# Attention, recurrence and a mixture of experts in one program: column halves at the end of each expert layer, row blocks for the input weights, expert rounds inside the pipeline, and a recurrent output product that starts with the front rows

## What is computed

```
h = x
for layer in (0, 1):
    hn = rms_norm(h, norm_mix[layer])
    h += attention(hn) if layer == 0 else recurrence(hn)
    h += mixture_of_experts(rms_norm(h, norm_ffn[layer]))
return rms_norm(h, final_norm)
```

## Time and profile before

| | us |
|---|---|
| median of 3 runs (lowest to highest) | 772.02 (771.46 to 773.8) |
| the profiled execution's own time | 769.73 |
| its span | 768.0 |
| PE busy | 641.2 (83%) |
| DVE busy | 315.9 (41%) |
| ACT busy | 224.2 (29%) |
| DMA, mean over the span | 321 GB/s, 246.15 MB |

### The profile page before, as it was taken

The page is one execution under the profiler, slowest core; times in us unless marked ns, Lnnn a source line. Parts: engine busy times, 40 slices in busy tenths (PEclk is TensorE's granted clock), DMA queues, the critical chain, the costliest instruction groups (busy, mean ns, idle before and its releaser), DMA issues.

```text
span 768.0 us, 11907 instructions
## 1 busy us (share of the span) xinstructions
PE 641.2 (83%) x4946; PEld 448.4 (58%) x4946; DVE 315.9 (41%) x533; ACT 224.2 (29%) x483; POOL 36.9 (5%) x62
## 2 busy tenths in 40 slices
PE   7999897999997595685879999989999985685775
PEld 6987786797453341331269999979965441332312
DVE  5555777545132211201375787742443311201204
ACT  4424654521121010110146666551211110110102
POOL 5100000000000100000000000050000000000000
PEclk9999999999999888987979999998999997987979
DMA  9993336578999999999993655529789999999993
GB/s 304 248 381 130 110 111 236 215 265 332 419 420 404 411 420 421 423 422 421 401 386 134 219 159 199 186 88 417 291 328 423 419 421 421 422 421 422 422 416 134
DMA packets 62580, 246.15 MB, mean 321 GB/s; under 512 B 4496, under 2 KB 12928, under 8 KB 41280
## 3 DMA queue, kind: packets, MB, share of 16 engines
q1 hardware_dynamic: 60896, 242.33, 80.5%
q0 software_dynamic: 992, 2.40, 1.0%
q10 hardware_dynamic: 640, 0.67, 0.3%
HBM read 244.34 MB, written 1.05 MB: 320 GB/s over the span
## 4 chain that ended last, share of the span: by engine, by line
PE 52%; DMA 28%; SPq 8%; DVE 6%; ACT 3%; issue 2%; DVEq 0%; ACTq 0%
DMA ring<-in_moe_w_down 19%; PE psum L2016 8%; PE psum L1673 8%; DMA ring<-in_moe_w_up 7%; PE psum L2073 7%; PE psum L1675 5%; PE psum L1682 4%; SPq L388 4%; PE psum L1684 3%; PE psum L1677 3%; SPq L437 2%; PE psum L2009 2%; PE psum L2000 2%; DMA ring<-in_att_w_in 2%; SPq L445 1%
## 5 line engine op out<-in xcount | busy, mean ns | idle before, releaser
L1421 DVE TENSOR_TENSOR arena<-psum,arena 128x256 f32<-128x256 f32 x16 | 6.8, 425 | 219.6 <-ACT arena L927 219.6
L2016 PE MATMUL psum<-arena,xT 128*32 128x512 f32 x512 | 64.7, 663 | 38.1 <-DMA arena<-in_moe_w_up 38.1
L2016 PE MATMUL psum<-ring,xT 128*32 128x512 f32 x512 | 66.4, 678 | 34.0 <-DMA ring<-in_moe_w_up 34.0
L2073 PE MATMUL psum<-ring,arena 128*32 128x512 f32 x464 | 59.4, 607 | 12.0 <-DMA ring<-in_moe_w_down 11.0
L1673 PE MATMUL psum<-x_hi,w_hi 128*128 128x256 f32 x256 | 65.8, 294 | 1.3 <-DVE x_hi L1110 0.6
L349 DVE TENSOR_TENSOR w_lo<-ring,w_hi 128x1024 fp32r<-128x1024 f32 x48 | 57.1, 1221 | 23.3 <-ACT w_hi L724 23.3
L923 ACT ACTIVATE arena<-psum 128x256 f32<-128x256 f32 x16 | 6.1, 383 | 207.1 <-PE psum L2016 207.1
L2016 PEld LDWEIGHTS psum<-arena,xT 128*32 128x32 f32 x512 | 17.7, 120 | 80.5 <-issue 45.2
L724 ACT ACTIVATE w_hi<-ring 128x1024 fp32r<-128x1024 f32 x48 | 49.0, 1052 | 47.7 <-PE psum L1684 28.1
L2016 PEld LDWEIGHTS psum<-ring,xT 128*32 128x32 f32 x512 | 17.0, 122 | 77.4 <-issue 42.2
L2009 PE MATMUL psum<-arena,xg 128*128 128x128 f32 x512 | 60.3, 276 | 0.7 <-DVE arena L1408 0.7
(11 more groups left out here) (313 smaller groups left out, 1037.9 us busy)
## 6 DMA issues: line engine op xcount, KB each, us to landing
ring<-in_moe_w_down SPq DMA_DIRECT2D x58, 1024.0 KB, 20.5
ring<-in_moe_w_gate SPq DMA_DIRECT2D x32, 1024.0 KB, 17.5
ring<-in_moe_w_up SPq DMA_DIRECT2D x32, 1024.0 KB, 19.6
arena<-in_moe_w_gate SPq DMA_DIRECT2D x32, 1024.0 KB, 23.1
arena<-in_moe_w_up SPq DMA_DIRECT2D x32, 1024.0 KB, 24.7
ring<-in_rec_w_in SPq DMA_DIRECT2D x16, 1024.0 KB, 13.6
ring<-in_att_w_in SPq DMA_DIRECT2D x8, 1024.0 KB, 12.7
ring<-in_att_w_out SPq DMA_DIRECT2D x4, 1024.0 KB, 10.6
```

Of the source, the lines that this page charges most:

```text
L2016: return pe.matmul(bank(3)[e * CAP:(e + 1) * CAP, :].rearrange("p (w f) -> p w f", w=2), gatheredT[:, k, e * CAP:(e + 1) * CAP], w, start= ...
L2073: last = pe.matmul(bank(5 + c)[e * CAP:(e + 1) * CAP, :], hidT[:, j, e * CAP:(e + 1) * CAP], down_part(l, kind, e, j)[:, c * 512:(c + 1) * ...
```

## The change

1. **Row blocks.** `cols` and the new `keys_values` give partition p the rows p, p+128, ... of the weight. The norms of the layers' inputs (v = 0 and 2) and the final one write straight; only the experts' norms keep the stride.
2. **Keys, values and gates** arrive as one block of 792 adjacent columns over two ring slots, in four DMAs. Their split waits for both slots. The low part of the `WG` columns moves to `ahead`, its split is two pieces on ACT and DVE instead of one, and the load of `U_VB` waits for three used units instead of two.
3. **First product.** DVE makes both low parts of `x` before the first low part of the weights; `first_quarter` starts with high x high when the first high part is there.
4. **Rounds.** `more` is read before the pipeline's loop on PE and ACT, whose loops now run to the last quad of the last round; the `If` of PE and ACT is gone. DVE and SP keep one, ahead of the last two (DVE) or the last (SP) quad.
5. **End of an expert layer.** `turn_hidden` of the last quad stands before the combine of the one before it. `down` signals its front half of columns (`down_front`) apart; `combine` goes by column half, then by row block, and starts with `y_front`. ACT squares each half of each row block as its adds finish (`norm_by_halves`); the first half's mean goes in as the bias of the logarithm.
6. **Recurrent output product.** For row block 0 DVE makes the high part too; PE runs the tile (0, 0) between the transposes of row block 0 and of row block 1. The order is then (1, 0), (0, 1), (1, 1), and m = 2, 3 as before.

```diff
 def cols(w, c0, n):
-    v = w.rearrange("(p k) n -> p k n", k=KD)[:, :, c0:c0 + n]
+    v = w.rearrange("(k p) n -> p k n", p=P)[:, :, c0:c0 + n]
...
+def keys_values(k0):
+    v = att.rearrange("(k p) n -> p k n", p=P)[:, :, C_KC:C_KC + KVW]
+    return [(lambda r, i=i: kvw[:, i:i + 2, :], v[:, i:i + 2, :]) for i in (k0, k0 + 2)]
-plan = [cols(att, 0, 512), blocks(512, (C_KC, 3 * P), (C_KW, P)),
-        blocks(WG, (C_VS, P), (C_VW, WG - P)),
+plan = [cols(att, 0, 512), keys_values(0), keys_values(KD // 2),
+RING_NEEDED[U_VB] = RING_NEEDED[U_WO]
...
 # DVE, norm
-if v < 2 * NL:
+if v % 2:
     rows = rows.rearrange("p (j k) -> p j k", k=KD)
 # PE
+def first_quarter(dst):
+    pe.wait_ge(s["w_high"], 1)
+    for k in range(KD):
+        pe.matmul(dst, quarter_hi(0)[:, k, :], x_hi[:, k, :], start=(k == 0), stop=False)
+    pe.wait_ge(s["x_lo_done"], TT)
+    for k in range(KD):
+        pe.matmul(dst, quarter_hi(0)[:, k, :], x_lo[:, :, k, :], start=False, stop=False)
+    pe.wait_ge(s["w_low_dve"], 1)
+    for k in range(KD):
+        last = pe.matmul(dst, q_lo[:, 0, k, :], x_hi[:, k, :], start=False, stop=(k == KD - 1))
...
 # PE, experts
+pe.wait_ge(s["passes_ready"], l + 1)
+more = pe.value_load(passes[l][0:1, 0:1], min_val=0, max_val=PASS_MAX - 1)
-with pe.Fori(2, NQ // 2) as i:
+with pe.Fori(2, (more + 1) * (NQ // 2)) as i:
     body(l, 2 * i, 0)
     body(l, 2 * i + 1, 1)
-pe.wait_ge(s["passes_ready"], l + 1)
-more = pe.value_load(passes[l][0:1, 0:1], min_val=0, max_val=PASS_MAX - 1)
-pe.wait_ge(s[f"added{l}"], 4 * NQ - 4)
-combine(l, NQ - 2)
-turn_hidden(l, NQ - 1)
-down(l, NQ - 1, last_quad=True)
-combine(l, NQ - 1)
+end = NQ * more + NQ - 1
+turn_hidden(l, end)
+pe.wait_ge(s[f"added{l}"], 4 * end)
+combine(l, end - 1)
+down(l, end, last_quad=True)
+pe.wait_ge(s[f"added{l}"], 4 * end + 4)
+combine(l, end)
 if l == 0:
     keep_clock(NORM, 3)
-with pe.If(more > 0):
-    with pe.Fori(0, more) as r:
...
 # PE, combine
-pe.wait_ge(s[f"y_rows{l}"], 2 * m + 2)
 for i, b in enumerate(COMBINE_BANKS):
-    t, half = divmod(i, 2)
+    half, t = divmod(i, 2)
+    if t == 0:
+        pe.wait_ge(s[f"y_back{l}" if half else f"y_front{l}"], m + 1)
...
 # ACT
+def norm_by_halves(l):
+    v = 2 * l + 2
+    for half in range(2):
+        for t in range(TT):
+            act.wait_ge(s["h_done"], H_NEEDED[v] + 2 * half + t + 1)
+            link(act.activation(square_moe[:, 0:512], h[:, t, half * 512:(half + 1) * 512], ACT.Square,
+                                accum_out=norm_part[:, l, t, half:half + 1]))
+            if half:
+                rstd(v, t, norm_part[:, l, t, 1:2], norm_part[:, l, t, 2:3])
+            else:
+                link(act.activation(norm_part[:, l, t, 2:3], norm_part[:, l, t, 0:1], ACT.Identity,
+                                    bias=eps_col[:, 0:1], scale=1.0 / D))
...
 # DVE, recurrence, inside the loop over row blocks, after the scaling of block t
+if t == 0:
+    for b in (0, 1):
+        dve.wait_ge(s["recT_psum"], b + 1)
+        dve.tensor_copy(rec_turned(mix_hi, b), bank(b).rearrange("p (k t) -> p k t", k=4))\
+            .then_inc(s["recT_high"], 1)
+    for b in (0, 1):
+        turned_low(b)
...
 # PE, recurrence, after the two transposes of row block t
+if t == 0:
+    pe.wait_ge(s["recT_high"], 2)
+    mix_tile(1, BASE_REC + 8, REC_BANKS, 0, (s["recT_low"], 2))
```

More of the change, by code:

```diff
@@ L566, in _ @@
                     with sp.Fori(0, more) as r:
[L567 to L573 removed]
+                        later_quad(NQ * r + NQ - 1, NQ - 1, 1, NQ - 2)
+                        later_quad(NQ * r + NQ, 0, 0, NQ - 1)
+                        with sp.Fori(0, NQ // 2 - 1) as i:
+                            n = NQ * (r + 1) + 2 * i
+                            later_quad(n + 1, 2 * i + 1, 1, 2 * i)
+                            later_quad(n + 2, 2 * i + 2, 0, 2 * i + 1)
+                end = NQ * more + NQ - 1
+                later_quad(end, NQ - 1, 1, NQ - 2)
+                sp.wait_ge(s[f"gate_up{l}"], end)
+                load_last_down(sp, l)
             for t in range(TT):
@@ L697, in hybrid_trunk @@
         COMBINE_BANKS = (7, 2, 0, 1)
-        H_NEEDED = [None, (7, 8), (10, 12), (19, 20), (22, 24)]
+        MIX_ORDER = ([(m, t) for m in range(4) for t in range(TT)],
+                     [(0, 0), (1, 0), (0, 1), (1, 1)] + [(m, t) for m in (2, 3) for t in range(TT)])
+        H_NEEDED = {2: 8, 4: 20}
         @block.scalar
@@ L771, in _ @@
             for t in range(TT):
-                norm(0, t, square)
+                norm(t)
             for t in range(TT):
@@ L978, in split_rec @@
                 split_high(BASE_REC, r)
-            for t in range(TT):
-                norm(2, t, square_moe)
+            norm_by_halves(0)
             for t in range(TT):
@@ L1307, in add_mix @@
                 v = 2 * l + 1
-                for m in range(4):
-                    for t in range(TT):
-                        c = slice(m * 256, (m + 1) * 256)
-                        dve.wait_ge(s["mix_psum"], 8 * l + 2 * m + t + 1)
-                        dve.tensor_tensor(h[:, t, c], bank(banks[m % 2 * 2 + t])[:, 0:256],
-                                          h[:, t, c], ALU.add).then_inc(s["h_done"], 1)
-                        if m == 3 and t == 0:
-                            norm(v, 0)
-                    if l == 0 and m < 2:
+                for i, (m, t) in enumerate(MIX_ORDER[l]):
+                    c = slice(m * 256, (m + 1) * 256)
+                    dve.wait_ge(s["mix_psum"], 8 * l + i + 1)
+                    dve.tensor_tensor(h[:, t, c], bank(banks[m % 2 * 2 + t])[:, 0:256],
+                                      h[:, t, c], ALU.add).then_inc(s["h_done"], 1)
+                    if m == 3 and t == 0:
+                        norm(v, 0)
+                    if l == 0 and m < 2 and t == TT - 1:
                         for r in (2 * m + 4, 2 * m + 5):
@@ L1969, in _ @@
             pe.wait_ge(s["sb_a"], SB_H)
-            mix(0, U_WO, (0, 1, 4, 5))
+            for i in range(len(MIX_ORDER[0])):
+                mix_tile(0, U_WO, (0, 1, 4, 5), i)
+            mix_end(0)
             def route(l):
@@ L2076, in down @@
                                              start=(j == 0), stop=(j == KF - 1))
-                last.then_inc(s[f"down{l}"], 1)
+                        if j == KF - 1:
+                            last.then_inc(s[f"down{l}" if c else f"down_front{l}"], 1)
             def body(l, n, parity, early=False):
```

291 lines of the change are left out of this document (137 added, 154 removed).

## The result

The changed kernel takes 757.61 us (median; 755.92 to 758.41) against 771.46 for the kernel before in the same session (769.69 to 773.8): a ratio of 0.982, with a 95% interval of 0.980 to 0.984. That is 13.9 us less. The forecast was 758.5 with a range of 755 to 765, forecast from a median of 772.02 for the kernel before. The profiled execution has a span of 753.9 us, against 768.0 before.

The account below looks back on a forecast made before the run. Expert weights' DMAs bound the expert streams, PE attention and recurrence; only time ahead of the streams or behind their last landings counts. -1.9 - 6.4 - 4.6 - 0.65 = -13.55 from the 772.02 median gives 758.5 us, range 755 to 765.

Parts of the forecast that it names:

- Start, -1.9: Kernel's start: straight norms and reordered first product give 1.4 us, kept because the QB weights land earlier; bounds 0 and -2.1.
- so 22.8: At the start: the new block of keys and values, 3.24 MB at 378 GB/s, lands at 22.8.
- The other half of the term: At the start: loading a block at 378 GB/s instead of small pieces at 256 lands the QB weights 2.1 us earlier.
- Clock between 50 and 60: In attention: the slow clock (0.83 granted, 1.7 us lost) may fall away or move; 1.7 either way in the range.
- End of layer 0's experts and start of the recurrence, -6.4: From combine to the recurrence's input product: earlier adds and norms, no PE "issue" stall, full clock; bounds -4.1 and 0.
- rival B: After layer 0's experts: PE's sequencer stalls all the same, -6.4 becomes 0, time 764.9; chance 0.12.
- Recurrent output product, -4.6: Behind the recurrence: second tile starts at 520.5 against 525.1; -2.8 if the clock falls as before.
- rival C: At the recurrence's start and its output product: the clock falls as before, +2.3 and +1.8, 762.6; chance 0.15.
- End of layer 1, -0.65: Last adds and norm: adds 1.0 earlier, last norm starts at 763.0 instead of 763.66; bounds -0.3 and -1.0.
- (a): Ahead of the saturated expert streams: time PE wins is passed on, with over 10 us of free transfer time each.
- D: At the start: QB weights land no earlier and the start's gain dies in the wait at 51.5; 760.4; chance 0.08.
- E: In the recurrence: row blocks of weights are read more slowly; at 130 GB/s the time is 787; chance 0.03.

Follow-up runs that it names:

- the kernel with pieces: Changed kernel with keys' and values' weights loaded in column pieces of 1536 and 512, then 512 and 608 bytes: 760.57 us, ratio 0.986.
- The two kernels that differ in this one branch: Changed kernel with TensorE's layer 0 `If` over a long block put back, 761.72 us; kernel before with that `If` and block taken out, 767.25.
- the kernel with the output product alone: Kernel before with only the recurrent output product's new order, tiles and DVE copies: 766.79 us, ratio 0.994.
- the reordered kernel: Changed kernel with stick-breaking scores of heads 4 and 5 computed behind the e products of heads 0 and 1: 756.93 us, ratio 0.982.
- the last kernel: Changed kernel with whole rows, scores of heads 4 and 5 behind e products, narrowed keys' block and 3 dummy matmuls: 754.75 us, ratio 0.979.

## Why the prediction was right, step by step

The total is right and no term has the wrong sign, but three of them are off, and they offset each other: the start fell short by 0.85, and the two ends gave 0.75 and 0.45 more. That the sum came within 0.6 of the measured span difference is in part luck. Shifts are read between the two profiles, spans 768.0 and 753.9.

**Start, -1.9: measured -1.05 at 51.** This pair of profiles gives the smallest difference that can be had: in seven profiles with the changed start the product behind the compressed branch comes at 49.70 to 50.49, in three with the old one at 51.55, 51.79 and 52.64. The norms and the first quarter came as forecast, the second quarter 0.34 late (ACT's first high part is at 14.41, not 14.21). The step that was mis-sized is the landing of the block, "so 22.8": it landed at 25.5. The forecast named the threshold itself, that a landing after 24.6 uses up the 2 us of cover; 0.57 of wait followed. I had given the block all of the 378 GB/s, but from 20 to 24 the rate was 265 and the MLP weights queued behind the block were already coming (from 22 to 24 the packets are 545 of 512 B and 21 of the block's 3168 B); they are slow ones, with 204 GB/s from 26 to 33, when the block is in. The other half of the term had the right cause and too large a size: QB landed at 43.1 (forecast 42.7), and the small pieces cost 1.4 (the kernel with pieces) to 1.7 (the kernel before), where I had 2.1. My 256 GB/s for them came from the stretch of 230, which also holds the MLP weights. In windows of the kernel before that part the two (length, busy PE, PEld, DVE, ACT, POOL, clock, DMA share, GB/s) the small pieces, 18 to 24, run at 293, and the MLP weights, 24 to 33, at 197:

```profile
18.00:24.00 6.00, 6.00 (x53) 6.00 (x52) 3.37 (x4) 1.51 (x3) 0.77 (x1) 1.00 1.18 293
24.00:33.00 9.00, 8.89 (x75) 8.67 (x74) 5.95 (x7) 5.06 (x5) 1.02 (x2) 1.00 1.21 197
```

At 293 the 1.67 MB take 5.7 us against 4.4: 1.3, near what was measured. The block moves at 391 from 14 to 20, so the case in which the pieces are no slower than the block (term 0, 760.4) did not come.

**Clock between 50 and 60, in the range as 1.7 either way.** The fall was absent in the profile (-1.5), and another at 131 gave it back (+1.5), so layer 0's stream starts 1.06 earlier. It is not shown to be an effect of the change: the same code showed either. That the two falls cancel in this pair of profiles is luck.

**End of layer 0's experts and start of the recurrence, -6.4: measured -7.15** (from 1.18 at 377.50 to 8.33, read at PE's product of L2206, 485.75 against 494.08). The second half of down takes 1.87 up to combine where I allowed 2.3, and the two low parts of x hold the first quarter up for 3.35, not 3.6. Everything else is within 0.2: transposes 6.7 behind combine (forecast 6.5), input product 10.35 behind it (10.4). The two kernels that differ in this one branch show that it was 4.7 to 5.5 of it, by the traces, and rival B is out. I had the bound right and its worth wrong: ACT's four steps do set the end, and that is why halves are 0.3 to 0.4 worse than whole rows here.

**Recurrent output product, -4.6: measured -4.8**, and -4.8 by itself on the kernel before. The clock stayed full; rival C did not come at either place.

**End of layer 1, -0.65: measured -1.1.** The first add is 1.4 earlier against the end of the stream's last wait (forecast 1.0), and the four steps take 0.34 of that back (forecast 0.35).

**Passed on?** The shift is 13.12 behind the output product and 13.2 at the last landing, so (a) held. Rivals D and E did not come: QB is earlier, and PE in the recurrence stands at nine tenths as before.

Sum of the measured terms: -1.05 - 0.0 (clock, one fall for another) - 7.15 - 4.8 - 1.1 = -14.1, and the span is shorter by 14.1. The straight norms, the new order of the first quarter and that of the last two quads were not run by themselves; their shares are read from the timelines.

**Open.** What decides where the clock falls in attention: idle pieces don't explain it alone (it fell where they were filled, too). Behind the start's 50 us, 11 of the 13 profiles have one fall in attention, the kernel with the output product alone has two (0.66 over 52 to 62, 0.87 over 128 to 138), and the first profile of the reordered kernel has none. And why 3.0 us won ahead of layer 1's stream shrank to 1.15 in one profile: two profiles of that same code need 122.7 and 121.3 from the first wait of the stream to the last, the changed kernel 120.8 in both. The loss is over early: the first wait for weights ends 2.14 earlier than in the changed kernel (599.48 to 601.62), the second 1.26 (610.32 to 611.58), and behind that it stays at 1.1 to 1.2. So a difference of 1.5 us between two single executions says nothing about a small edit. The trace between two fixed points does, where the same stretch in other profiles of the same code repeats: combine to input product is 10.35 in four profiles with halves, while the start scatters by 0.8.

## What to carry to other kernels

Look at "issue" idle at the first instruction behind a branch: a never-entered block that is long cost 4 us here and the clock behind it, and the same branch over a short block cost nothing; put rare work in a loop whose trip count grows instead. Before a step is cut in halves, count the steps of the engine that ends last: two short ones with their accumulator reads were longer than one long one. For a transfer that gets larger, work out its landing with what shares the queues in its last third, and hold that against the cover.

## What the runs showed of the hardware

- A jump over a block of two quads' products: 4.09 us of "issue" (4.19 in the kernel before); over one instruction: none (the 0.78 is DVE's norm).
- TensorE's clock fell to 0.5 (1.2 of 2.4 GHz) at places that differ between executions of the same code: at 54 to 58 or at 131 to 134, for 1.5 us of loss; behind 1.78 and 0.77 us of idle it stayed at 0.50 for all of 52 to 62 and cost 4.1. In the last kernel it fell with no idle piece over 0.17 us ahead, in the middle of 32 products of 15 columns (1.00 in the us from 51, 0.90 from 52, 0.50 from 53). The same 32 products stand in every kernel, and in the changed one's first profile the clock is 1.00 over them.
- A float32 product of 128 columns is two records of PE: 38 for 19 dummies, 4.7 us together.
- The squares of half rows on ACT: 0.63 and a 0.19 accumulator read for 512 columns, 1.06 and 0.19 for 1024.
- Weights in pieces of 512 and 608 B over all partitions moved at 293 GB/s (18 to 24 us of the kernel before), the block's 3168 B pieces at 391 (14 to 20 us of the changed kernel), the MLP's 512 B pieces, each to half of the partitions, at 197 to 206 (24 to 33 us of either).
